# A two-block transformer kernel on one core: norm chains at the seams in halves of 512 columns

## The reference, cut to what matters

```
def rms_norm(x, g):
    xf = x.astype(jnp.float32)
    y = xf * lax.rsqrt(jnp.mean(xf * xf, axis=-1, keepdims=True) + EPS)
    return (y * g.astype(jnp.float32)).astype(x.dtype)
...
x = x + 0.5 * swiglu_ffn(rms_norm(x, ffn1_norm[l]), ffn1_w13[l], ffn1_w2[l])
h = rms_norm(x, mix_norm[l]); proj = h @ w_in[l]
...
x = x + y @ w_out[l]
x = x + 0.5 * swiglu_ffn(rms_norm(x, ffn2_norm[l]), ffn2_w13[l], ffn2_w2[l])
return rms_norm(x, final_norm)
...
h = h + gdn_mixer(hn, ...)
h = h + swiglu(rms_norm_2(h, ln_ffn[i]), ffn_w_in[i], ffn_w_out[i])
h = h + (p[i] @ ple_w_proj[i]) * jax.nn.sigmoid(rms_norm_2(h, ln_ple[i]) @ ple_w_gate[i])
k_sh, v_sh = shared_kv(h, kv_norm, w_kv, k_norm)
...
h = h + sb_mixer(hn, k_sh, v_sh, ...)
```

## Time and profile before

| | us |
|---|---|
| median of 3 runs | 1328.08 |
| all three | 1327.57, 1328.08, 1331.91 |
| the profiled execution's own time | 1331.8 |
| its span, first to last instruction | 1330.1 |
| busy in the span: PE, DVE, ACT, POOL | 1276.0, 756.7, 615.5, 73.8 |
| granted clock of TensorE, mean | 0.982 of full |

### The profile page before, as it was taken

One profiled execution on the slowest core, in us unless ns is written; L12 is line 12 of the kernel. 1 busy time (PEld: TensorE's weight loads), 2 busy tenths in 40 slices (PEclk: granted clock), 3 DMA queues, 4 the chain that ended last, 5 costly groups with the idle time before them and its releaser, 6 DMA issues.

```text
span 1330.1 us, 16393 instructions
## 1 busy us (share of the span) xinstructions
PE 1276.0 (96%) x6711; PEld 1088.6 (82%) x6711; DVE 756.7 (57%) x852; ACT 615.5 (46%) x766; POOL 73.8 (6%) x125
## 2 busy tenths in 40 slices
PE   8999999988999999999999999999999989999997
PEld 6888888987788887899998788888777767888886
DVE  4655435983655545677775755544676426555434
ACT  5544326744444433556513544433554735444323
POOL 1000002001100001100001100000122001000001
PEclk9999999989999999899999999999998999999999
DMA  8865547340766564445102566554445406665530
GB/s 270 272 190 190 191 147 231 123 125 0 220 192 190 184 213 141 159 137 197 33 1 64 171 216 202 168 189 170 174 159 189 143 0 199 199 196 189 190 127 32
DMA packets 140140, 212.27 MB, mean 160 GB/s; under 512 B 10234, under 2 KB 101246, under 8 KB 140061
## 3 DMA queue, kind: packets, MB, share of 16 engines
q1 hardware_dynamic: 140064, 211.22, 48.8%
HBM read 210.14 MB, written 1.05 MB: 159 GB/s over the span
## 4 chain that ended last, share of the span: by engine, by line
PE 88%; DVE 5%; ACT 3%; POOL 1%; issue 1%; DMA 0%; SPq 0%; ACTq 0%; POOLq 0%
PE bank L1477 25%; PE bank L1479 25%; PE bank L1478 25%; DVE wlo L978 2%; PE bank L1866 2%; PE bank L1604 1%; PE bank L1877 1%; PE bank L1500 1%; ACT whi L376 1%; DVE xTlo L999 1%; PE bank L1722 1%; DVE X L1022 1%; PE bank L1885 1%; POOL krs L877 1%; PE bank L1837 1%
## 5 line engine op out<-in xcount | busy, mean ns | idle before, releaser
L978 DVE TENSOR_TENSOR wlo<-raw,whi 128x2048 fp32r<-128x2048 f32 x190 | 433.9, 2290 | 295.2 <-ACT whi L376 294.9
L376 ACT ACTIVATE whi<-raw 128x2048 fp32r<-128x2048 f32 x190 | 362.2, 1913 | 236.5 <-PE bank L1479 227.2
L1477 PE MATMUL bank<-whi,xThi 128*128 128x512 f32 x1024 | 408.7, 399 | 19.8 <-DVE xTlo L999 7.2
L1479 PE MATMUL bank<-whi,xTlo 128*128 128x512 f32 x1024 | 401.6, 392 | 0.0
L1478 PE MATMUL bank<-wlo,xThi 128*128 128x512 f32 x1024 | 401.3, 392 | 0.0
L1477 PEld LDWEIGHTS bank<-whi,xThi 128*128 128x128 f32 x1024 | 193.9, 189 | 64.7 <-DVE wlo L978 9.4
L1479 PEld LDWEIGHTS bank<-whi,xTlo 128*128 128x128 f32 x1024 | 193.8, 189 | 41.5
L1478 PEld LDWEIGHTS bank<-wlo,xThi 128*128 128x128 f32 x1024 | 194.2, 190 | 38.4
L1477 PE MATMUL bank<-whi,hThi 128*128 128x512 f32 x352 | 138.1, 392 | 0.0
L1479 PE MATMUL bank<-whi,hTlo 128*128 128x512 f32 x352 | 137.2, 390 | 0.0
L1478 PE MATMUL bank<-wlo,hThi 128*128 128x512 f32 x352 | 137.0, 389 | 0.0
(11 more groups left out here) (388 smaller groups left out, 1216.0 us busy)
## 6 DMA issues: line engine op xcount, KB each, us to landing
raw<-in_ffn_w_dram SPq DMA_DIRECT2D x176, 256.0 KB, 4.1
raw<-in_ffn_w_in_dram SPq DMA_DIRECT2D x176, 256.0 KB, 4.0
raw<-in_ffn_w_dram SPq DMA_DIRECT2D x22, 1024.0 KB, 4.9
raw<-in_ffn_w_out_dram SPq DMA_DIRECT2D x22, 1024.0 KB, 5.0
raw<-in_gdn_w_in_dram SPq DMA_DIRECT2D x16, 1024.0 KB, 5.5
raw<-in_w_in_dram SPq DMA_DIRECT2D x10, 1024.0 KB, 5.2
raw<-in_ple_w_gate_dram SPq DMA_DIRECT2D x8, 1024.0 KB, 5.0
raw<-in_w_kv_dram SPq DMA_DIRECT2D x8, 1024.0 KB, 6.4
```

The source lines that it names most:

```text
L376: act.activation(whi[w % SPLIT][:], raw[w % RAW][:], ACT.Copy).then_inc(w_hi, 1)
L978: dve.tensor_tensor(wlo[w % SPLIT][:], raw[w % RAW][:], whi[w % SPLIT][:].bitcast(F32), ALU.subtract).then_inc(w_lo, 1)
L1477: pe.matmul(psum, lhs[0], rhs[0], start=start, stop=False, skip_group_check=True)
L1479: return pe.matmul(psum, lhs[1], rhs[0], start=False, stop=stop, skip_group_check=True)
```

## The change

- In the last slot of every `wide` weight PE finishes one bank (six matmuls) before it starts the other, and signals `wide_half` after it. DVE's adds and ACT's sigmoids wait for their own bank.
- `x_ready`, `gate_s` and `turn_in` count halves of 512 columns. ACT squares half by half into two sums (scaled by 1/sqrt(D)); POOL adds the two and EPS. DVE scales half by half, PE transposes half by half, and PE waits for the half of xTlo that its slot reads. The add after a gate runs by halves too. The first norm and the second of two at `gdn` keep whole sums.
- For the slots 1 to `ahead - 1` of the eight weights behind a seam (`HALVED`, 17 slots), DVE forms wlo in two instructions of 1024 columns and signals `w_half` after the first. PE starts such a slot on `w_half` and waits for the whole at its middle.
- At `gdn` wlo of slot 1 moves behind `add(1)`. Ahead of the `up` weights the transposes of tile 1 move up by three matmuls. At `gdn_out` the turn starts after four of eight heads. At `sb_out` the transposes of tile 0 start after half the heads, and those of tile 1 move behind the first slot of tile 0.
- The result is stored in four DMAs of 128 x 512 instead of two of 128 x 1024.

```diff
+        HALVED = sorted(first[x] + i for x in ("mix", "up1", "gdn", "up2", "ple_g0", "kv", "up3", "ple_g1")
+                        for i in range(1, ahead(x)))
+
+        def half_split(w):
+            return (w_half, HALVED.index(w) + 1) if w in HALVED else (w_lo, split_done(w))
+
...
+            return 4 * [x for x in TURN if x != "sb"].index(name) + 2 * t + b + 1
+
+        def added(m, t, b=1):
+            return 4 * m + 2 * t + b + 1
 
...
-
-            if t == 0:
+                for b in range(2):
+                    c = slice(b * 512, (b + 1) * 512)
+                    sp.wait_ge(sem("x_ready"), added(len(WIDE) - 1, t, b))
+                    sp.dma_start(out[0, t * P:(t + 1) * P, c], X[:, t, c]).then_inc(sem("stored"), 16)
+            sp.wait_ge(sem("stored"), 2 * 16 * NT)
+
+        def wait_wide(eng, m, t, b):
+
+            if b == 0:
+                eng.wait_ge(sem("wide_half"), 2 * m + t + 1)
+            elif t == 0:
                 eng.wait_ge(sem("wide_mm0"), m + 1)
             else:
...
+                    act.activation(junk, (xs if n == FINAL + 1 else X)[:, t, :], ACT.Square,
+                                   accum_out=sumsq[:, 2 * n + t, 0:1]).then_inc(sem("norm_ss"), 1)
+                    return
+                for b in range(2):
+                    c = slice(b * 512, (b + 1) * 512)
+                    if b:
+                        act.wait_ge(ready, value)
+                    ins = act.activation(junk[:, c], X[:, t, c], ACT.Square, scale=1.0 / ROOT_D, accum_out=sumsq[:, 2 * n + t, b:b + 1])
+                ins.then_inc(sem("norm_ss"), 1)
 
             def turn_hi(name, t, dst=None):
...
-                    wait_wide(act, m, t)
                     for h in range(2):
-                        ins = act.activation(gate_s[:, t, h * 512:(h + 1) * 512], out_bank(t, h)[:], ACT.Sigmoid)
-                    ins.then_inc(sem("gate_s"), 1)
+                        wait_wide(act, m, t, h)
+                        act.activation(gate_s[:, t, h * 512:(h + 1) * 512], out_bank(t, h)[:], ACT.Sigmoid).then_inc(sem("gate_s"), 1)
                 return gate
 
...
-                    root(rstd[:, c], meansq[:, c], sumsq[:, c], D, ("norm_ss", "norm_rstd"), nth(n, t))
+                    if n == 0:
+                        root(rstd[:, c], meansq[:, c], sumsq[:, c, 0], D, ("norm_ss", "norm_rstd"), nth(n, t))
+                        continue
+                    pool.wait_ge(sem("norm_ss"), nth(n, t))
+                    step(pool.tensor_scalar(meansq[:, c], sumsq[:, 2 * n + t, 0:1], sumsq[:, 2 * n + t, 1:2], EPS, ALU.add, ALU.add))
+                    pool.tensor_tensor(rstd[:, c], meansq[:, c], half[:, 0:1], ALU.pow).then_inc(sem("norm_rstd"), 1)
 
             def mixer1():
...
-                    dve.tensor_tensor(wlo[w % SPLIT][:], raw[w % RAW][:], whi[w % SPLIT][:].bitcast(F32),
+                    if w in HALVED:
+                        c = slice(0, SLOT // 2)
+                        dve.tensor_tensor(wlo[w % SPLIT][:, c], raw[w % RAW][:, c], whi[w % SPLIT][:, c].bitcast(F32),
+                                          ALU.subtract).then_inc(w_half, 1)
+                    c = slice(SLOT // 2 if w in HALVED else 0, SLOT)
+                    dve.tensor_tensor(wlo[w % SPLIT][:, c], raw[w % RAW][:, c], whi[w % SPLIT][:, c].bitcast(F32),
                                       ALU.subtract).then_inc(w_lo, 1)
...
-                dve.scalar_tensor_tensor(out=xs[:, t, :], in0=X[:, t, :], scalar=rstd[:, c:c + 1],
-                                         in1=gain[n % 2][:], op0=ALU.mult, op1=ALU.mult).then_inc(sem("turn_in"), 1)
+                for b in range(2):
+                    part = slice(b * 512, (b + 1) * 512)
+                    dve.scalar_tensor_tensor(out=xs[:, t, part], in0=X[:, t, part], scalar=rstd[:, c:c + 1], in1=gain[n % 2][:, part],
+                                             op0=ALU.mult, op1=ALU.mult).then_inc(sem("turn_in"), 1)
 
             def turn_lo(name, t, hi=None, lo=None):
...
                 for t in range(NT):
-                    if t and n in (4, 7):
+                    if t and n == 7:
                         split(first[follows] + 2)
...
                     for h in range(2):
-                        ins = dve.scalar_tensor_tensor(
+                        wait_wide(dve, m, t, h)
+                        dve.scalar_tensor_tensor(
                             out=X[:, t, h * 512:(h + 1) * 512], in0=out_bank(t, h)[:], scalar=scale,
-                            in1=X[:, t, h * 512:(h + 1) * 512], op0=ALU.mult, op1=ALU.add)
-                    ins.then_inc(sem("x_ready"), 1)
+                            in1=X[:, t, h * 512:(h + 1) * 512], op0=ALU.mult, op1=ALU.add).then_inc(sem("x_ready"), 1)
                 split(last_group(name) + SPLIT)
                 return add
...
-                dve.wait_ge(sem("x_ready"), 2 * 2 + t + 1)
+                if t:
+                    split(first["gdn"] + 2)
+                dve.wait_ge(sem("x_ready"), added(2, t))
...
-            def rows(w, t, src, k0, nk, psums, begins, ends, only=None):
-
-                for k in only or range(nk):
-                    for c, psum in enumerate(psums):
-                        at = (k * len(psums) + c) * 512
-                        ins = passes(psum[:], [x[:, k0 + k, t * P:(t + 1) * P] for x in src],
-                                     [x[:, at:at + 512] for x in ring(w)], begins and k == 0, ends and k == nk - 1)
+            def rows(w, t, src, k0, nk, psums, begins, ends, only=None, by_bank=None):
+
+                order = [(k, c) for k in only or range(nk) for c in range(len(psums))]
+                if by_bank:
+                    order.sort(key=lambda x: x[1])
+                for n, (k, c) in enumerate(order):
+                    if t == 0 and k == nk // 2 and w in HALVED:
+                        pe.wait_ge(w_lo, split_done(w))
+                    at = (k * len(psums) + c) * 512
+                    ins = passes(psums[c][:], [x[:, k0 + k, t * P:(t + 1) * P] for x in src],
+                                 [x[:, at:at + 512] for x in ring(w)], begins and k == 0, ends and k == nk - 1)
+                    if by_bank and n == nk - 1:
+                        ins.then_inc(by_bank, 1)
                 return ins
 
-            def turn_T(name, t, wait=None):
-                pe.wait_ge(*(wait or (sem("turn_in"), turned_in(name, t))))
+            def turn_T(name, t):
                 for b in range(2):
+                    pe.wait_ge(*((sem("sb_o_in"), 2 * b + 2) if name == "sb" else (sem("turn_in"), turned_in(name, t, b))))
                     before = 4 * turn(name) + 2 * t + b - 1
                     if before > 0:
...
-            def turned(name, t):
-                pe.wait_ge(sem("turn_lo"), 4 * turn(name) + 2 * t + 2)
+            def turned(name, t, b=1):
+                pe.wait_ge(sem("turn_lo"), 4 * turn(name) + 2 * t + b + 1)
 
...
+                        if i < 2:
+                            turned(name, t, i)
                         if t == 0:
-                            pe.wait_ge(w_lo, split_done(s + i))
+                            pe.wait_ge(*half_split(s + i))
                         for k in range(4):
-                            if (i, t, k) == (2, 0, 3):
+                            if (i, t, k) == (2, 0, 2):
                                 turn_T(name, 1)
                             ins = rows(s + i, t, xT, 4 * (i % 2), 4, [bank[2 * (i // 2) + t]], i % 2 == 0, i % 2 == 1, (k,))
                         if t:
@@ -1620,10 +1668,8 @@
                         elif i % 2:
                             ins.then_inc(sem("ffn_mm0"), 1)
 
-                    turned(name, 0)
                     for i in range(3):
                         part(i, 0)
-                    turned(name, 1)
                     for i in range(3):
                         part(i, 1)
...
-            def one_tile_first(name):
+            def one_tile_first(name, beside=3):
                 def ready(i, t):
-                    if (i, t) == (0, 0):
-                        turned(name, 0)
-                    if (i, t) == (3, 0):
+                    if i % 2 == 0:
+                        turned(name, t, i // 2)
+                    if (i, t) == (beside, 0):
                         turn_T(name, 1)
-                    if (i, t) == (0, 1):
-                        turned(name, 1)
                 return ready
 
...
-
-                def ready(i):
-                    if i == 0:
-                        for t in range(NT):
-                            turned("sb", t)
-                return ready
+                turn_T("sb", 0)
+                return one_tile_first("sb", 1)
 
 
             def next_turn(name):
                 return lambda: turn_T(name, 0)
```

70 lines of the change are left out of this document (34 added, 36 removed).

## The result

The changed kernel took 1313.4 us (median of four runs, 1312.4 to 1314.3); the kernel before, run beside it, 1327.8. The ratio is 0.9887, 95% interval 0.9862 to 0.9911. The forecast was 1306.5, range 1302 to 1312: the direction was right, the gain 14.5 us where 21 were expected. The profiled execution took 1312.4, span 1310.7, against 1331.8 and 1330.1 before: 19.4 less, where the sum said 25.8.

A forecast was written before the change was run, and what follows sets the result against it. TensorE, busy 1276.0 of 1330.1 us, was taken as the bound, so only its waits counted. Savings by place summed to 25.8 us off 1331.8, 1306.0, plus 0.5 for thin margins: 1306.5 us, range 1302 to 1312.

The forecast's parts named there:

- What lies beside other work, at nothing: Everywhere: extra halves of slots, squares and scalings, and new waits, are hidden beside other work; priced at nothing.
- mix: Seam at mix: the wlo stop goes (1.13) and the xTlo stop falls from 1.57 to 0.95; 1.8 us saved.
- up2 and up3: Tile 1 ahead of up2 and up3: the wlo stop (1.13) and xTlo stop (1.15) go; 2.3 us saved each.
- sb_out and gdn_out: Fewer stops and moved transposes at sb_out, 2.7 us; four transposes starting during gdn_out's second four heads, 0.4 us.
- kv: Seam at kv: wlo stop falls from 1.29 to 0.5, the next grows from 0.92 to 1.3; 0.4 us saved.
- up1's tile 0: Ahead of up1, tile 0: stop of 2.12 falls to 0.6 and the half clock behind it goes; 3.0 us saved.
- Gdn: Seam at gdn: matmuls start 2.9 us sooner and 2.9 of half clock goes; 5.8 us, bounds 1.8 and 6.0.
- Up1, tile 1: Ahead of up1, tile 1: the wlo stop (1.13) and the xTlo stop (1.15) go; 2.3 us saved.
- ple_g0 and ple_g1: Seams at ple_g0 and ple_g1: stops of 1.13 + 0.64 become about 0.25; 1.5 us saved each.
- Rival 2: GpSimd and VectorE get in each other's way, POOL holding DVE at six places, 4.4 us: 1311 us; chance 0.12.
- The end: Behind the last product: first half done in the shade saves 1.45, smaller last store 0.3; 1.8 us saved.
- Rival 1: Idle time goes, but the 1.2 GHz clock stays at gdn (3.0) and up1 (1.7) or moves: 1311 us; chance 0.17.

The follow-up runs named there:

- b_odd: The kernel before with an unused 32-byte tensor behind sumsq and no instruction changed: 1334.3 us, ratio 1.0059.
- a_256: The changed kernel with 160 unused bytes behind sumsq, so hThi and hTlo start 256 bytes later than before: 1309.4 us, ratio 0.9873.
- a_256_2: a_256 repeated, beside a repeat of the changed kernel on one chip: 1310.4 us.
- after_2: The changed kernel itself, repeated beside a_256_2 on one chip: 1311.3 us.
- a_one: a_256 with ScalarE instead of POOL adding the two half sums for token tile 1 of every norm from n1 on: 1305.6 us at equal clock, median 1309.4.
- u_store: a_256 with each token tile stored whole (512 KB) behind the last addition: median 1311.1 us; last VectorE operation to end of span 3.06 us for 2.45.
- few: a_256 with neither wlo slots nor squares taken by halves: 1306.3 us, ratio 0.9838.

## Why the prediction was right and wrong

**What failed: the edit that wasn't priced.** It is the line with sumsq. "What lies beside other work, at nothing" lists halved slots, squares, scalings and waits; the larger tensor has no term at all. It shifted hThi and hTlo by 96 bytes against the slots and cost 7.9 us on the engine that is busy in 97% of the span. No rival covers it. b_odd shows such a shift alone (32 bytes, 5.9 us at equal clock), a_256 takes it away (8.0 us).

Without it the forecast would still have been 3 to 4 us short: a_256 and a_256_2 took 1309.4 and 1310.4. 25.8 less 22.4, so 3.4 us, are missing at the seams (below). And the 22.4 can't be taken off the median as they are, which would give 1305.4: 4.6 of them are clock (1.7 at up1, 2.9 at gdn), and the mean clock of these kernels is 0.987, that of the kernel before. 1327.8 less 17.8 is 1310.0, which is what they took.

**Right:** mix 1.7 for 1.8, up2 and up3 4.2 for 4.6, sb_out and gdn_out 3.1 for 3.1, kv 0.3 for 0.4 (its wait for xs grew from 0.92 to 1.06, where the signs said past 1.1), up1's tile 0 2.8 for 3.0: the transposes wait 0.71 where 0.6 was foreseen, with POOL in 0.30 and 0.56:

```profile
326.61 0.30 POOL L909 TENSOR_SCALAR meansq<-sumsq 128x1 f32<-128x1 f32 x1 [15.79 <-ACT xs L414]
...
328.45 1.27 PE L1545 MATMUL bank<-ident,xs 128*128 128x128 f32 x8 [0.71 <-issue]
```

**Gdn, 5.5 for 5.8:** counted from the end of the wide product (521.8 here, 524.5 before) the transposes begin after 7.3 us and the matmuls after 9.4, where 7.1 and 9.1 were foreseen and 8.6 and 12.0 stood before. The stops are 1.82 and 0.75 for 3.18 and 1.41, and the clock stayed at 1.00 behind them in this execution:

```profile
529.11 1.32 PE L1545 MATMUL bank<-ident,xs 128*128 128x128 f32 x8 [1.82 <-DVE xs L1026]
531.18 0.50 PE L1516 MATMUL bank<-whi,xThi 128*128 128x512 f32 x1 [0.75 <-DVE xTlo L1034]
```

In after_2 it fell there for 3.4 us, which costs 1.7. The forecast called this its least sure term, and rightly; that this profile shows nearly all of it is luck.

**Up1, tile 1, short by 1.0, ple_g0 and ple_g1 by 0.8 each.** The steps took rstd for ready when VectorE came to the scaling. Ahead of up1 POOL's first step took 3.03 us, through three half subtractions; first POOL, then VectorE:

```profile
335.29 3.03 POOL L909 TENSOR_SCALAR meansq<-sumsq 128x1 f32<-128x1 f32 x1 [7.73 <-ACT xs L414]
```
```profile
334.65 1.23 DVE L1011 TENSOR_TENSOR wlo<-raw,whi 128x1024 fp32r<-128x1024 f32 x1
335.79 1.23 DVE L1008 TENSOR_TENSOR wlo<-raw,whi 128x1024 fp32r<-128x1024 f32 x1
336.92 1.23 DVE L1011 TENSOR_TENSOR wlo<-raw,whi 128x1024 fp32r<-128x1024 f32 x1
339.00 1.41 DVE L1026 SCALAR_TENSOR_TENSOR xs<-X,rstd,gain 128x512 f32<-128x512 f32 x2 [0.85 <-POOL rstd L910]
```

and at ple_g0 both steps were held, so that VectorE stood idle for 0.45 us and TensorE for 0.65:

```profile
931.97 1.88 POOL L909 TENSOR_SCALAR meansq<-sumsq 128x1 f32<-128x1 f32 x1 [14.18 <-ACT xs L414]
...
933.94 1.39 POOL L910 TENSOR_TENSOR rstd<-meansq,half 128x1 f32<-128x1 f32 x1
...
935.36 1.41 DVE L1026 SCALAR_TENSOR_TENSOR xs<-X,rstd,gain 128x512 f32<-128x512 f32 x2 [0.45 <-POOL rstd L910]
...
936.21 1.05 PE L1545 MATMUL bank<-ident,xs 128*128 128x128 f32 x6 [0.65 <-issue]
```

The sign named, "POOL's rstd is under 1.7 us everywhere", held (1.40 at most); it watched the second step, and the first was held. Rival 2 had the partners right and the direction wrong: POOL waits, and VectorE's halves start 1.13 us apart with or without it. The rule of the Trainium skill (page SBUF — State Buffer, section SBUF: two separate sides), that the one who comes second is blocked for the whole instruction, fits POOL here but not by how much, since POOL let two ends of VectorE's operations pass at up1 and one at ple_g0. For ple_g0 and ple_g1 a_one shows the cause: with the sum ready sooner the stops fall to 0.14. For up1 it is read from the traces alone, since a_one's own step was held there.

**The end, 2.1 for 1.8.** The smaller last store saves 0.6, not 0.3; the interpolation between landing times of loads was too low, within its bounds. The Trainium skill's fixed 2.0 us and 436 GB/s (page DMA: Bandwidth & Descriptors, section Anatomy of one DMA — SWDGE (gpsimd) path) gave 0.6, and u_store agrees with 0.62; the page gives them for DMAs that GpSimd issues, and these are issued by SyncE.

**The clock.** The forecast took the same number for the profiled run and the median, since the profiled run of before had the slower clock (0.982) that the change would take away. They came out alike, 1312.4 and 1313.4, but in part by luck: some 10 of the 25.6 us of slow clock that went in the profiled pair lay neither at up1 nor at gdn nor at the end. Rival 1 (1311) named a near number for another reason than the one that made the kernel slow. Its mechanism, a slow clock that stays or turns up elsewhere, fits the kernels with the distance restored: up1's slow stretch is gone in every profile behind the change, but gdn's stood in one of the changed kernel's two and in six of their seven.

**Parts priced together that the runs took apart.** Halved wlo carry 2.7 us at equal clock and lose it again to the clock, squares by halves lose 1.2 to 1.8, the bank order is worth 0.7, the stores 0.6. The additions, scalings and transposes by halves and the moved instructions (at gdn, the up seams, gdn_out and sb_out) were not undone alone; what is left of 17.5 us at equal clock falls to them together, if the parts add up, which no run tests.

## What to carry to other kernels

When a diff changes a tensor's size, price the new places too: print the starts before and after, and compare the starts of what TensorE multiplies. A stop that is halved on paper should be costed after the other edits have moved its start, not from the old trace. Compare small differences at equal mean clock as well as by the medians, and keep the version that the medians favour, here the one with fewer edits (few), though its interval overlaps that of a_256.

## What was not expected of the hardware

- The pace of 128x128 by 128x512 matmuls depends on the distance between the starts of stationary and moving tensor within a partition: 227.1 ns where it is a multiple of 256 bytes, 229.3 to 234.2 at the other seven distances tried, at full clock, with the weight loads lasting 188 ns all the same. With 256 columns and the roles exchanged a distance of 192 is better than none, 114.5 for 119.9 ns.
- A 128x1 step of POOL that takes 0.30 us alone took 1.49 to 3.03 beside back-to-back VectorE subtractions of 1.22 us.
- The mean granted clock of a kernel differs by 0.004 to 0.005 between versions that differ by the halving of 17 subtractions (0.991 and 0.992 for 0.987), 5 us in 1310. How that comes about was not found.
